# Merging the two products with the high weight part in the up pieces of four dense layers of a 1-core transformer kernel

## What is computed

```python
def squared_relu_mlp(h, w_up, w_down):          # hidden 4096
    u = jax.nn.relu(h @ w_up)
    return (u * u) @ w_down

def conv_ffn(h, w_up, conv_w, conv_b, w_down):  # hidden 2816, w_up is (1024, 5632)
    u = h @ w_up
    up = jnp.pad(u, ((0, 0), (2, 0), (0, 0)))
    u = conv_b + up[:, 0:S] * conv_w[0] + up[:, 1:1 + S] * conv_w[1] + up[:, 2:2 + S] * conv_w[2]
    gate, val = jnp.split(u, 2, axis=-1)
    return (jax.nn.silu(gate) * val) @ w_down
```

## Time and profile before

| | us |
|---|---|
| median of 3 runs | 1347.53 |
| lowest, highest | 1346.55, 1347.55 |
| the profiled execution, its own time | 1348.96 |
| its span in the profile | 1347.2 |
| PE busy in the span | 1329.0 (99%) |
| DVE busy | 910.1 (68%) |
| ACT busy | 727.5 (54%) |

### The profile page before, as it was taken

How to read it: one execution, slowest core, us unless ns; L and a number is a source line. 1 busy time by engine, 2 the same in 40 slices (tenths; PEclk the granted TensorE clock), 3 DMA queues, 4 the chain that set the end, 5 groups by cost and what they waited for, 6 DMA issues and landing times.

```text
span 1347.2 us, 23075 instructions
## 1 busy us (share of the span) xinstructions
PE 1329.0 (99%) x8792; PEld 1190.3 (88%) x8792; DVE 910.1 (68%) x1421; ACT 727.5 (54%) x1160; POOL 121.7 (9%) x123
## 2 busy tenths in 40 slices
PE   9999999999999999999999999999999999999998
PEld 8887999988987789999989889999989876999996
DVE  5766655557744657555568768877768975787776
ACT  6555544445343546444466347655557755665553
POOL 0101000001500100000001310000003233000000
PEclk9999999999999999999999999999999999999999
DMA  7535656565553465656545345555555421465551
GB/s 254 169 132 200 229 178 198 177 198 168 193 191 126 154 222 170 201 175 202 174 145 201 126 158 178 182 187 186 185 177 189 160 77 52 135 205 186 187 189 65
DMA packets 64031, 231.77 MB, mean 172 GB/s; under 512 B 7104, under 2 KB 7360, under 8 KB 63936
## 3 DMA queue, kind: packets, MB, share of 16 engines
q1 hardware_dynamic: 62208, 224.42, 49.8%
q10 hardware_dynamic: 1728, 6.00, 1.3%
HBM read 229.34 MB, written 1.05 MB: 171 GB/s over the span
## 4 chain that ended last, share of the span: by engine, by line
PE 89%; DVE 6%; ACT 3%; issue 1%; DMA 1%; POOLq 0%; SPq 0%; POOL 0%; DVEq 0%; ACTq 0%
PE ps L571 27%; PE ps L573 27%; PE ps L572 27%; DVE w_lo L1735 1%; DVE x_lo L1755 1%; DMA ring<-ws 1%; PE ps L942 1%; PE ps L1134 1%; ACT w_hi L1239 1%; DVE arena L2319 1%; PE ps L543 1%; PE ps L865 1%; PE ps L790 0%; ACT x_hi L1261 0%; PE ps L1103 0%
## 5 line engine op out<-in xcount | busy, mean ns | idle before, releaser
L1735 DVE TENSOR_TENSOR w_lo<-ring,w_hi 128x1024 fp32r<-128x1024 f32 x423 | 514.2, 1254 | 167.7 <-ACT w_hi L1239 167.2
L1239 ACT ACTIVATE w_hi<-ring 128x1024 fp32r<-128x1024 f32 x423 | 428.6, 1054 | 233.3 <-PE ps L573 176.3
L571 PE MATMUL ps<-x_hi,w_hi 128*128 128x256 f32 x1600 | 454.7, 284 | 0.5 <-DVE x_lo L1755 0.5
L573 PE MATMUL ps<-x_hi,w_lo 128*128 128x256 f32 x1600 | 452.7, 283 | 0.0
L572 PE MATMUL ps<-x_lo,w_hi 128*128 128x256 f32 x1600 | 452.7, 283 | 0.0
L571 PEld LDWEIGHTS ps<-x_hi,w_hi 128*128 128x128 f32 x1600 | 306.8, 192 | 3.7 <-issue 2.7
L572 PEld LDWEIGHTS ps<-x_lo,w_hi 128*128 128x128 f32 x1600 | 306.9, 192 | 1.0
L573 PEld LDWEIGHTS ps<-x_hi,w_lo 128*128 128x128 f32 x1600 | 306.8, 192 | 0.0
L571 PE MATMUL ps<-w_hi,y_hi 128*128 128x512 f32 x560 | 220.3, 393 | 0.4 <-DVE y_lo L1787 0.4
L572 PE MATMUL ps<-w_lo,y_hi 128*128 128x512 f32 x560 | 218.3, 390 | 0.0
L573 PE MATMUL ps<-w_hi,y_lo 128*128 128x512 f32 x560 | 218.1, 389 | 0.0
(11 more groups left out here) (224 smaller groups left out, 1246.2 us busy)
## 6 DMA issues: line engine op xcount, KB each, us to landing
ring<-ws SPq DMA_DIRECT2D x424, 512.0 KB, 4.9
tab<-tables ACTq DMA_DIRECT2D x3, 572.0 KB, 5.7
rowg<-rows ACTq DMA_DIRECT2D x3, 512.0 KB, 6.5
h<-x SPq DMA_DIRECT2D x4, 256.0 KB, 6.5
out<-arena SPq DMA_DIRECT2D x4, 256.0 KB, 2.2
arena<-decay ACTq DMA_DIRECT2D x1, 768.0 KB, 9.5
sm<-small ACTq DMA_DIRECT2D x1, 642.0 KB, 6.1
arena<-narrow ACTq DMA_DIRECT2D x1, 512.0 KB, 6.6
```

Source lines behind the costliest of these rows:

```text
L571: mm(o, lh, rh, start=start, stop=False, skip_group_check=True)
L573: return mm(o, ll, rh, start=False, stop=stop, skip_group_check=True)
L1239: A(w_hi[:, q // 2 % RING, c:c + HALF], ring[:, q % RAW, :], ACT.Copy).then_inc(hi_ready, 1)
L1735: V.tensor_tensor(w_lo[:, g % RING, v], ring[:, q % RAW, :], w_hi[:, g % RING, v].bitcast(F32), ALU.subtract).then_inc(lo_ready, 1)
```

## The change

All of it stands in the four dense layers.

- `x_hi` and `x_lo` become two parts of one tensor `x_both`, side by side for each input block. A new function `wide` takes the place of `transposed` and `first_unit` in `hidden`. For each triple it issues one matmul with the high weights and both parts of x (512 moving columns, a full bank) and one with the low weights and the high part (256 columns), which is added onto the upper half of the bank. The large term stands then in columns 0 to 255, and the two small terms in columns 256 to 511.
- A unit takes two banks (`pair_bank`): units 0 and 1 the banks 0 to 3, later ones in turn 4 and 5, or 6 and 7. From unit 4 on, unit u waits until unit u-2 has been read out.
- ACT copies the small terms of both banks out of PSUM. DVE adds them to the large terms, which releases the banks. In an MLP, DVE then applies ReLU and square in one operation, and ACT copies the square to `y_hi`. In a feed-forward, DVE then multiplies by the token scales as an operation of its own.
- In a feed-forward, ACT applies SiLU for unit u-1 behind the copy for unit u, and its two halves of the weight refill stand ahead of and behind the bases and `y_hi`, where both stood together behind them.
- The scales' transposes go to bank 6, and unit 3 waits until they are copied.

```diff
-        x_hi, x_lo = sb("x_hi", [P, KT, T], F32R), sb("x_lo", [P, KT, T], F32R)
+        x_both = sb("x_both", [P, KT, 2, T], F32R)
+        x_hi, x_lo = x_both[:, :, 0, :], x_both[:, :, 1, :]
...
+        def pair_bank(u):
+            return 2 * u if u < 2 else 4 + 2 * (u % 2)
...
+            def wide(g, b, first=None, mid=None):
+                s = g % RING
+                for part, j in [(e, j) for e in range(2) for j in range(2)] if first is not None else [(None, 0), (None, 1)]:
+                    if j == 1 and mid is not None:
+                        mid()
+                    for k in range(KT) if part is None else (lower, upper)[part]:
+                        if j == 0 and k % 4 == 0:
+                            split(g, k // 4)
+                        if j == 0 and first is not None:
+                            x_tiles(first, k)
+                        c = k * 256 + j * P
+                        mm(ps[:, b + j, :], w_hi[:, s, c:c + P], x_both[:, k, :, :], start=k == 0, stop=False,
+                           skip_group_check=True)
+                        r = mm(ps[:, b + j, T:2 * T], w_lo[:, s, c:c + P], x_hi[:, k, :], start=False, stop=k == KT - 1,
+                               skip_group_check=True)
+                    if (part, j) == (0, 0):
+                        turn_over(first, 1, part=upper)
+                r.then_inc(done, 1)
...
                     for u in (2 * c, 2 * c + 1):
-                        if u >= 6:
-                            pe.wait_ge(freed, at + u - 3)
-                        if u == 0:
-                            first_unit(st.up(c), bank(u), n)
-                        else:
-                            transposed(st.up(c) + u % 2, bank(u),
-                                       mid=(lambda: spread(n)) if u == 1 and n in SCALE_OF else None)
+                        if u >= 4:
+                            pe.wait_ge(freed, at + u - 1)
+                        if u == 3 and n in SCALE_OF:
+                            pe.wait_ge(scale_ready, SCALE_OF[n] + 1)
+                        wide(st.up(c) + u % 2, pair_bank(u), first=n if u == 0 else None,
+                             mid=(lambda: spread(n, 6)) if u == 1 and n in SCALE_OF else None)
```

ACT, in `mlp` and `ffn`:

```diff
-                            act.wait_ge(ready, u - 1)
-                        A(relu[:, u % 2, :], ps[:, bank(u), :], ACT.Relu).then_inc(freed, 1)
-                        act.wait_ge(freed, u + 1)
+                            act.wait_ge(sq, at + u - 1)
+                        A(relu[:, u % 2, :].rearrange("p (a t) -> p a t", t=T), ps[:, b:b + 2, T:2 * T], ACT.Copy)\
+                            .then_inc(low, 1)
+                        act.wait_ge(sq, at + u + 1)
-                        A(y_hi[:, i:i + 2, :], relu[:, u % 2, :].rearrange("p (a t) -> p a t", t=T), ACT.Square)\
+                        A(y_hi[:, i:i + 2, :], square[:, u % 2, :].rearrange("p (a t) -> p a t", t=T), ACT.Copy)\
                             .then_inc(hh, 1)
...
-                        act.wait_ge(freed, at + u + 1)
+                        g, b = st.up(c) + u % 2, pair_bank(u)
+                        act.wait_ge(done, g + 1)
+                        if u >= 2:
+                            act.wait_ge(freed, at + u - 1)
+                        A(conv_small[:, u % 2, :, :], ps[:, b:b + 2, T:2 * T], ACT.Copy).then_inc(low, 1)
+                        if u:
+                            gate(u - 1)
+                        if g + RING < G_END:
+                            hi_half(2 * (g + RING))
+                        act.wait_ge(scaled_in, at + u + 1)
                         for e in range(2):
                             r = A(conv[:, u % 2, e, :], conv_in[:, u % 2, e, :], ACT.Identity,
                                   scale=par(u, 4 + e), bias=par(u, 6 + e))
                         r.then_inc(base, 1)
                         if u:
                             product_hi(u - 1)
-                        refill(st.up(c) + u % 2)
-                        act.wait_ge(conv_done, at + u + 1)
-                        A(silu[:, u % 2, :], conv[:, u % 2, 0, :], ACT.Silu).then_inc(sl, 1)
+                        if g + RING < G_END:
+                            hi_half(2 * (g + RING) + 1)
                     if u == units - 1:
+                        gate(u)
                         product_hi(u)
```

DVE, in `mlp` and `ffn`:

```diff
-                        dve.wait_ge(freed, u + 1)
-                        v = relu[:, u % 2, :]
-                        V.tensor_tensor(square[:, u % 2, :], v, v, ALU.mult).then_inc(sq, 1)
+                        dve.wait_ge(low, at + u + 1)
+                        v, b = relu[:, u % 2, :], pair_bank(u)
+                        o = v.rearrange("p (a t) -> p a t", t=T)
+                        V.tensor_tensor(o, ps[:, b:b + 2, 0:T], o, ALU.add).then_inc(freed, 1)
+                        dve.wait_ge(freed, at + u + 1)
+                        V.scalar_tensor_tensor(square[:, u % 2, :], v, 0.0, v, ALU.max, ALU.mult).then_inc(sq, 1)
...
-                        dve.wait_ge(done, g + 1)
-                        scaled(conv_in[:, u % 2, :, :], ps[:, bank(u), :], scale).then_inc(freed, 1)
+                        dve.wait_ge(low, at + u + 1)
+                        b, v = pair_bank(u), conv_in[:, u % 2, :, :]
+                        V.tensor_tensor(v, ps[:, b:b + 2, 0:T], conv_small[:, u % 2, :, :], ALU.add).then_inc(freed, 1)
+                        dve.wait_ge(freed, at + u + 1)
+                        V.tensor_tensor(v, v, scale.unsqueeze(1).broadcast_to([P, 2, T]), ALU.mult).then_inc(scaled_in, 1)
```

36 lines of the change are left out of this document (21 added, 15 removed).

## The result

The changed kernel takes **1354.78 us** at the median of 12 runs (1348.97 to 1359.27), the kernel before 1347.72 in the runs beside it (12 runs, 1346.55 to 1350.98): a ratio of 1.0046, 95% interval 1.0036 to 1.0057. It is slower by 7.1 us by the medians and 6.2 by the ratio (4.9 to 7.7), where 14.7 us of gain were forecast. The profiled execution took 1357.86 us, span 1356.1.

The account below looks back on a forecast made before the run. PE, busy 99% of the span, was taken as the bound, so its instruction pitch counts. Gain -15.8, first units +0.4, opening stalls +0.7 sum to -14.7 us: 1332.8 us at the median, range 1330 to 1335 (0.66), 1330 to 1340.5 (0.80).

Parts of the forecast that it names:

- PE's gain, 1216 x 13.0 = 15.8 us: MLPs and feed-forwards: each of 1216 triples loses one matmul instruction, worth 13.0 ns, 15.8 us in all.
- The rival that the merged matmul gives back less: PE's merged units: large matmul's weight load doesn't fit behind the small one; 1340.5 to 1347.5 us, chance 0.08.
- The border that I read a mixed pitch from: Border of down and up on PE: small matmul behind a large one, 208.24 to 208.35, no longer than the rest.
- The Trainium skill's 2.5 ns: PE's matmuls: skill page's gap between isolated warm matmuls; one instruction less worth 2.5 ns, whole change 3.0 us.
- MLPs at no cost: MLPs: ACT's copy and DVE's extra operation cost nothing, since the down pieces cover them.
- DVE's unit 5.96 us: Feed-forwards: DVE's unit grows from 5.25 by 0.71 to 5.96 us, against PE's 5.54.
- The 0.7 us of stall in the opening: Opening units of both feed-forwards: PE waits for banks because DVE falls back; 0.7 us together, ends 0 and 2.
- DVE 14.2 us, PE 16.5 us, so it catches up and PE sets the pace: Feed-forward chunks after the opening, two units and one down piece: DVE needs 14.2 us, PE 16.5, so lateness shrinks.
- So the half that is moved ahead of the bases costs nothing; its cover is 1.5 us: ACT's queue in feed-forward units: the weight half lands early enough for the bases, with 1.5 us to spare.
- End of the layer, 8.3 us against two down pieces, 10.9: Feed-forward end: last `y_lo` comes about 8.3 us after the last unit; two down pieces, 10.9 us, cover it.
- The rival "the feed-forward becomes a loop of ACT and DVE": Feed-forwards: late transfers delay ACT, then DVE, then the next transfers; 1352.9 us, slower than before, chance 0.04.

Follow-up runs that it names:

- e2_act_behind: Changed kernel with ACT's feed-forward refill behind a down piece put after the next unit's copy and SiLU, that unit's first half behind `y_hi`: 1339.79 us.
- e8_halves_behind: Changed kernel with both weight halves of a feed-forward unit put back behind the bases and `y_hi` on ACT: 1348.84 us.

## Why the prediction was wrong, point by point

- **PE's gain, 1216 x 13.0 = 15.8 us: a size that was off.** The pitches of one kind do add up, but for a pair that holds only at one of its two pitches; 68 of 76 units were at the other, 353 in place of 346.5, so that the gain was 1216 x 13.0 less 6.9, some 9 us. The rival that the merged matmul gives back less was half right: I gave as its reason a weight load that doesn't fit; the loads take the same time at both pitches, and no run tests that reason. The border that I read a mixed pitch from the earlier trace rows has a large matmul ahead of a small one once, and a small one ahead of a large one never.
- **The Trainium skill's 2.5 ns** ("TensorE: Matmul & The Clock Gate", Back-to-back issue gap), which it gives for isolated matmuls, would have put 3.0 us in place of the 15.8, an estimate from that page. The traces don't bear it out for these matmuls with a weight load each: a triple's instruction less is worth 13.0 ns at one pitch and 6.5 at the other.
- **MLPs at no cost: right.** No wait in them; 1.8 us gained in each.
- **DVE's unit 5.96 us: right** (5.97). **The 0.7 us of stall in the opening did not come:** PE waits for no add there, in either feed-forward. The add of unit 5 is 4.2 and 4.0 us late, where 4.6 and up to 5.8 were forecast; the slower pitch gave DVE 0.1 us more per unit, but e2_act_behind, whose openings run at the forecast pitch, has no such wait either (4.5 in both).
- **"DVE 14.2 us, PE 16.5 us, so it catches up and PE sets the pace": the step that failed.** 14.2 is the sum of DVE's work. It takes for granted that DVE's input is there when DVE is. With the waits DVE moves on by 17.2 us a chunk against PE's 16.8. The input no longer came from PE but through ACT's queue, and I looked up what stands behind the new copy and not what stands ahead of it at the one place where that differs: behind a down piece, where the refill waits for the ring. Moving that refill (e2_act_behind) brings the catch-up back.
- **"So the half that is moved ahead of the bases costs nothing; its cover is 1.5 us": wrong.** The cover was worked out from transfers that are issued in time. With DVE 5 us late they aren't, and this half lengthens the loop (e8_halves_behind: 5.9 us).
- **End of the layer, 8.3 us against two down pieces, 10.9: right in its terms, wrong in its start.** Those 8.3 us allow for an add that starts 0.6 us behind the unit; the chain from the add is 7.93 as against my 7.7, and the add was 7.71 us late.
- **The rival "the feed-forward becomes a loop of ACT and DVE", 0.04, 1352.9 us: this is what came**, with its mechanism, through another door. I let it decide at a DVE unit of 7.35 us, by transfers of 7 us or more. It needed neither: its units stayed at 5.97 in the opening, the transfers' median at 5.0, and the lost time lay in one wait per chunk. The loss came out in the form of one wait at the end, with the clock's fall on top, which I had not priced. That its number lies within 2 us of the result is luck: it had 5.9 us lost in a layer's chunks and 4.5 in its opening, and neither is there.

The parts together, for the first feed-forward of the profiled execution. Up to the end of unit 21 PE takes 163.5 us in place of 165.7, so 2.1 are saved (22 x 0.1, less about 0.03 on each of seven down pieces). The wait at the end costs 4.98 - 0.23 = 4.75. Eight matmuls at the low clock take 3.5 in place of 1.8, 1.7 more; the rest of the closing down pieces 0.5 more. Just behind the layer 0.9 are lost, 0.8 of them in a wait of PE for DVE's `h`. The sum is +5.8, as measured. In the second the same terms are -2.1, 4.4 and 2.9 (14 matmuls), 5.2 of 5.3.

## What to carry over

When an operation is put on an engine that takes its instructions in order, as ACT's rows show here, so that another engine depends on it, list what stands *ahead* of it on that queue at each kind of place in the loop, and ask of each whether it can wait for a transfer: a short copy behind a conversion that waits for its data is held as long as the transfer is late. A sum of busy times below the bound's period doesn't say that an engine catches up; find the loop that its inputs make, and compare that loop's period. And give a small lag its end: lateness that nobody waits for in the middle of a layer is paid where the cover runs out, here with a lower clock behind it.

## What the runs showed of the hardware that was not expected

- One and the same alternation of a 512-column and a 256-column matmul runs at 346.7 or at 353 ns a pair at a full granted clock (1.00 in the windows), and keeps its speed for whole units. Down pieces right behind a unit at 353 take longer too (5.50 in place of 5.45 us). Uniform runs show one speed (226.7, 119.8). Two large and two small in turn stay at 348. What selects the pitch is open; it is neither the form of the operand, nor the half of the bank, nor a down piece ahead alone.
- At PE's waits at the ends of the feed-forwards, 4.6 and 4.2 us, the granted clock fell to 1.2 GHz, and the matmuls behind them ran at it for 3.5 us in the first and some 6 us in the second (windows at 0.64, 0.50 and 0.77). In e8_halves_behind it stayed at 1.00 behind a wait of 2.6 us and fell behind one of 2.4 us, so the length of the wait alone doesn't tell. Its price in the median run is open: filler that held the clock gained 1.5 us, its own 4.3 us per layer included.
